# A sum of two weight quarters made by an accumulating GpSimd DMA instead of a VectorE add

## The chip, the core and the metric

One core of one Trainium2 chip runs the whole program. The metric is the device time of one launch in microseconds (us); lower is better. TensorE multiplies, VectorE (DVE), ScalarE (ACT) and GpSimd (POOL) work on data in SBUF and PSUM, and DMA queues bring data from HBM; SyncE (SP) issues nearly all of the loads.

## What is computed

Two layers of a streaming encoder over 528 tokens (16 meta tokens and 512 real ones) with 1024 channels. Each layer is a gated feed-forward network (FFN), a mixer and a second FFN. So there are four FFNs, and they hold most of the work:

```python
def swiglu(h, w_gate, w_up, w_down):
    return (jax.nn.silu(h @ w_gate) * (h @ w_up)) @ w_down
...
    for layer in range(DEPTH):
        g = norm_gains[layer]
        h = h + 0.5 * swiglu(rmsnorm(h, g[0]), ffn_w_gate[layer, 0], ffn_w_up[layer, 0], ffn_w_down[layer, 0])
        u = rmsnorm(h, g[1])
...
        h = h + mix
        h = h + 0.5 * swiglu(rmsnorm(h, g[2]), ffn_w_gate[layer, 1], ffn_w_up[layer, 1], ffn_w_down[layer, 1])
    return rmsnorm(h, final_norm)[:, N_META:]
```

`D_FF` is 2816, in 22 blocks of 128 columns. All data is float32.

## The kernel before

**Groups.** The gate and up products of an FFN go in two passes, `groups(q, p)` for FFN `q` = 0 to 3 and half `p` = 0 or 1; behind each pass stands `down(q, p)`, the part of the down projection that it feeds. A pass works on groups of two blocks of `D_FF`. A pass with `p` = 0 has five groups, one with `p` = 1 has six; the very first pass has two. The first group of a pass is the one that `leads(g)` names. In a group, each weight matrix (gate, and up beside it) is cut into four quarters `a11`, `a21`, `a22`, `a12` of 128 by 1024 in SBUF, and seven products take the place of eight: `p1` takes `a11`, `p2` takes `a12`, `p4` takes `a22`, and four take sums of quarters: `p7` takes `s3 = a11 + a21` (line 1252 or 1255), `p5` takes `s1 = a21 + a22` (line 1270), `p6` takes `s2 = a11 + s1` (line 1276) and `p3` takes `s4 = a12 + s2` (line 1303). Each product is made once for the gate (`n = 2g`) and once for up (`n = 2g + 1`), so a group holds 14.

**Splits.** A weight that TensorE reads is held as a high part, which ScalarE copies into a shorter float type (`wh`; functions `high_...`), and a low part, the difference, which VectorE makes (`wl`; functions `low_...`). A product is 12 matmuls: four pieces of the contraction, three parts each. So each of the six forms costs a ScalarE copy and a VectorE difference, and the four sums cost a VectorE add each.

**Buffers.** The quarters arrive in a ring of four slots, `raw`. In every group but the first of a pass, `s3` goes to the scratch row `ws[:, 5]`, `s1` is then added in place onto `a21` in `raw`, `s2` in place onto `a11`, and `s4` into another row of `ws`. SyncE loads a quarter of the next group into a slot as soon as its old content is done with: `a11` behind `s4`, `a21` behind `low_s1`, `a22` behind `low_a22`, `a12` behind `p2`.

**Order.** There is no scheduler: each engine's list is written by hand, and semaphores that count tie them. In an inner group `g` VectorE goes through `low_s2(g)`, `low_s1(g)`, `sum_s4(g)`, the split of `a12`, work on PSUM results and on the hidden rows, `low_s4(g)`, `low_a22(g)`, `low_a11(g+1)`, `sum_s3(g+1)`, `gate_a_out(g)` (1456), `sum_s1(g+1)`, `sum_s2(g+1)`, `low_s3(g+1)`, `c21` (1452), `gate_b_scale` (1466), and in the next round `c22` (1445). TensorE's order in an inner group is `p1(n)`, `p7(n)`, `p3(n-1)`, `p6(n)`, `p4(n-1)`, `p2(n)`, `p5(n)`, `p1(n+1)`, `p7(n+1)`, `p3(n)`, `p6(n+1)`, `p4(n)`, `p2(n+1)`, `p5(n+1)`. ScalarE goes, from the middle of the group: `high_s3` (623), three PSUM copies, the silu of the gate (804), `high_s2(g+1)` (630), the second silu (810), `high_s1(g+1)` (638), `p1_copy` (721), the split of `a12` (661).

**What `p6(n)` waits for.** `s2_low` (the low part of `s2`) and `p1_copied` (ScalarE's copy at line 721, which stands behind `high_s1` in its list). GpSimd's list in the FFNs holds only `clear_ss`, a memset of the row of squares, which waits for the norm before it.

Of the kernel before, what the change touches and what calls it, by code (L numbers as in the profile page):

```python
# [6 lines left out]
ALU = mybir.AluOpType  # L7
# [18 lines left out]
CHUNKS_UP = 2 * FT  # L26
# [59 lines left out]
def leads(g):  # L86

    return g == GROUP[PASS_OF[g]][0]
# [22 lines left out]
def leading(g):  # L111

    return sum(leads(h) for h in range(g + 1))


def ring_place(kind, g):
# [88 lines left out]
def trunk(nc, x_dram, gains, w_gu, w_dn, ev_in, ev_out, od_in, od_out, conv_w, sinks, rel_bias, gate_b, pool_w,  # L205
          pool_scale, ident_in, onehot_in, causal_in, sel_in, out):
    table_dram = nc.dram_tensor("bias_table", [P, 8, TABLE], F32, kind="Internal").ap()
    with ExitStack() as ctx:
# [3 lines left out]
        def sem(name):  # L212
            return ctx.enter_context(nc.semaphore(name))
# [174 lines left out]
        form_ready, first_ready, u_added = sem("form_ready"), sem("first_ready"), sem("u_added")  # L388
        down_front, down_back, down_scaled = sem("down_front"), sem("down_back"), sem("down_scaled")
        table_kept = sem("table_kept")  # L390
        a12_split, b21_split = sem("a12_split"), sem("b21_split")

        block = ctx.enter_context(nc.Block())
# [181 lines left out]
        def _(act):  # L575
# [54 lines left out]
                act.activation(wh[:, form_slot("s2", g), :], raw_quarter("a11", g), ACT.Copy).then_inc(s2_high, 1)  # L630

            def high_s1(g):
                act.wait_ge(s1_sum, g + 1)
                if leads(g):
                    act.activation(wh[:, 5, :], ws[:, 5, :], ACT.Copy).then_inc(s1_high, 1)
                else:
                    act.wait_ge(p7_done if leads(g - 1) else p5_done, 2 * g)
                    act.activation(wh[:, form_slot("s1", g), :], raw_quarter("a21", g), ACT.Copy).then_inc(s1_high, 1)

# [488 lines left out]
        def _(pool):  # L1128
# [8 lines left out]
            def clear_ss(v):  # L1137
                if v:
                    pool.wait_ge(stat_done, v)
                pool.memset(ss[:, :], 0.0).then_inc(ss_zero, 1)  # L1140
                pool.wait_ge(ss_zero, v + 1)

            clear_ss(0)
            clear_ss(1)

            pool.memset(zbuf[:, 0:2], 0.0).then_inc(pool_step, 1)
            steps[0] += 1
            pool.wait_ge(pool_step, steps[0])
            for s in range(EV_TILES):
# [14 lines left out]
                if s >= 7 and (s - 7) % 3 == 0:  # L1164
                    j = (s - 7) // 3
                    pool.wait_ge(acc_free, TILE["ev_in"] + s + 1)
                    pool.tensor_tensor(zbuf[:, 2:2 + L], conv_c[:, :], conv_x[:, :], ALU.mult).then_inc(z_ready, 1)
            clear_ss(2)
            clear_ss(3)
            clear_ss(4)  # L1170

            for s in range(OD_TILES):
# [27 lines left out]
                                       ALU.subtract).then_inc(pool_ready, 1)  # L1200
            pool.wait_ge(yd_l, 4)
            clear_ss(5)
            clear_ss(6)
            pool.wait_ge(x_gained, KT - 1)
            for h, (a, b) in enumerate(ENDS):
# [6 lines left out]
        def _(dve):  # L1212
# [34 lines left out]
            def sum_s3(g):  # L1247
                dve.wait_ge(raw_in[raw_slot("a11", g)], RAW_COUNT["a11", g])
                dve.wait_ge(raw_in[raw_slot("a21", g)], RAW_COUNT["a21", g])
                if leads(g):  # L1250
                    dve.wait_ge(s1_sum, g + 1)
                    dve.tensor_tensor(raw_quarter("a21", g), raw_quarter("a11", g), raw_quarter("a21", g), ALU.add).then_inc(s3_sum, 1)
                else:
                    dve.wait_ge(p5_done if leads(g - 1) else p7_done, 2 * g)
                    dve.tensor_tensor(ws[:, 5, :], raw_quarter("a11", g), raw_quarter("a21", g), ALU.add).then_inc(s3_sum, 1)
# [7 lines left out]
            def sum_s1(g):  # L1263
                dve.wait_ge(raw_in[raw_slot("a21", g)], RAW_COUNT["a21", g])
                dve.wait_ge(raw_in[raw_slot("a22", g)], RAW_COUNT["a22", g])
                if not leads(g):
                    dve.wait_ge(s3_sum, g + 1)
                elif g:
                    dve.wait_ge(p7_done, 2 * g)
                dve.tensor_tensor(s1_full(g), raw_quarter("a21", g), raw_quarter("a22", g), ALU.add).then_inc(s1_sum, 1)  # L1270

            def sum_s2(g):
                dve.wait_ge(s1_sum, g + 1)
                dve.wait_ge(s3_sum, g + 1)
                dve.wait_ge(a11_low, g + 1)
                dve.tensor_tensor(raw_quarter("a11", g), raw_quarter("a11", g), s1_full(g), ALU.add).then_inc(s2_sum, 1)
# [209 lines left out]
            def groups(q, p):  # L1486
# [4 lines left out]
                for g in range(first, end):  # L1491
                    if g == first:
                        low_a22(g)
                        low_a11(g + 1)
                        sum_s3(g + 1)
                        if q and not p:
                            norm(V_FFN[q], real)
                        sum_s1(g + 1)
                        if p:
                            sum_s2(g + 1)  # L1500
                        c22(2 * g, real)
                        c22(2 * g + 1, real)
                        if not p:
                            sum_s2(g + 1)
                        c21(2 * g, real)
                        low_s3(g + 1)
                        gate_a_out(g, real)
                        low_s2(g + 1)
                        c21(2 * g + 1, real)
                        gate_b_scale(g, real)  # L1510
                        continue
# [21 lines left out]
                        sum_s3(g + 1)  # L1533
                    gate_a_out(g, real)
                    if g + 1 < end:
                        sum_s1(g + 1)
                        sum_s2(g + 1)
                        low_s3(g + 1)
                    else:
                        low(n)  # L1540
                    c21(2 * g, real)
                    gate_b_scale(g, real)
                    if q and not p and g == first + 1:
                        low_b21(q, real)
# [1083 lines left out]
```

## Time and profile before

| | before |
|---|---|
| median of 3 runs | 1822.62 us (1822.48 to 1823.01) |
| the profiled execution, first to last instruction (span) | 1821.0 us |
| busy: TensorE, VectorE, ScalarE, GpSimd | 1801.7, 1344.8, 859.6, 53.1 us |
| granted TensorE clock, mean | 0.998 of full |
| `in_w_gate_up` quarter loads issued by SyncE | 175 of 512 KB |

No device time of the profiled execution is given apart from its span; the median of the runs lies 1.6 us above that span. A timeline row gives the start, the duration, the engine, the line and the tiles; brackets hold the idle time of that engine just before it and what ended it. Starts of neighbouring VectorE rows are less than a duration apart, because the next instruction starts while the last one ends.

### The profile page before, as it was taken

The page shows a single profiled execution, that of the slowest core. Times are in us where ns is not written, and L with a number is a line of the kernel's source. Part 1 is how long each engine was busy: PE and PEld are TensorE (multiplying, and loading weights), DVE is VectorE, ACT ScalarE, POOL GpSimd, SP SyncE. Part 2 cuts the span into 40 slices and gives each one's busy share as a digit, 9 for nine tenths or more (in the row PEclk, how much of TensorE's full clock was granted, in tenths as well). Part 3 has the DMA queues.
Part 4 walks back from the last instruction along what each step waited for, and adds up shares of the span by engine and source line. Part 5 has one row for each costly group of instructions (what it writes and reads, how often), then busy time and mean ns, then how long its engine had stood idle before and what let it go on. Part 6 is the DMA issues. An engine that isn't in the chain of part 4 may idle for free.

```text
span 1821.0 us, 32718 instructions
## 1 busy us (share of the span) xinstructions
PE 1801.7 (99%) x13456; PEld 1720.7 (94%) x13456; DVE 1344.8 (74%) x1814; ACT 859.6 (47%) x1404; POOL 53.1 (3%) x68
## 2 busy tenths in 40 slices
PE   8999999999999999999999999999999999999997
PEld 8999999999999999999999999999998899889986
DVE  7766887557778966896798578855656799568954
ACT  8443464335446543554555335534423565335542
POOL 0000000000000000000000000000124000000000
PEclk9999999999999999999999999999999999999999
DMA  5255233341222333233223322333312223332331
GB/s 179 85 96 116 95 115 108 102 135 59 70 70 82 101 99 108 89 105 105 82 93 108 97 98 97 107 112 112 93 59 70 70 82 105 102 106 93 111 111 57
DMA packets 81107, 176.87 MB, mean 97 GB/s; under 512 B 7292, under 2 KB 12700, under 8 KB 80960
## 3 DMA queue, kind: packets, MB, share of 16 engines
q1 hardware_dynamic: 80544, 174.49, 31.3%
q8 instruction: 108, 1.77, 0.4%
q14 instruction: 39, 0.32, 0.1%
q10 hardware_dynamic: 416, 0.29, 0.0%
HBM read 171.35 MB, written 3.41 MB: 96 GB/s over the span
## 4 chain that ended last, share of the span: by engine, by line
PE 96%; DVE 2%; ACT 1%; DMA 0%; SPq 0%; issue 0%; DVEq 0%; ACTq 0%
PE psum L2028 25%; PE psum L2098 13%; PE psum L2100 13%; PE psum L2101 13%; PE psum L2038 7%; PE psum L2037 4%; PE psum L2041 4%; PE psum L2036 4%; PE psum L2040 3%; PE psum L2148 2%; PE psum L2147 2%; PE psum L2149 2%; PE psum L2157 2%; DMA rb_sb<-in_rel_bias 0%; DVE rms L1391 0%; PE psum L2336 0%
## 5 line engine op out<-in xcount | busy, mean ns | idle before, releaser
L2098 PE MATMUL psum<-fh,wh 128*128 128x264 f32 (+1 forms) x1968 | 559.9, 285 | 2.2 <-ACT psum L728 2.2
L2101 PE MATMUL psum<-fh,wl 128*128 128x264 f32 (+1 forms) x1968 | 557.2, 283 | 0.0
L2100 PE MATMUL psum<-fl,wh 128*128 128x264 f32 (+1 forms) x1968 | 556.7, 283 | 0.0
L2098 PEld LDWEIGHTS psum<-fh,wh 128*128 128x128 f32 x1968 | 371.1, 189 | 3.5 <-issue 3.0
L2100 PEld LDWEIGHTS psum<-fl,wh 128*128 128x128 f32 x1968 | 370.9, 188 | 0.6
L2101 PEld LDWEIGHTS psum<-fh,wl 128*128 128x128 f32 x1968 | 369.8, 188 | 0.0
L588 ACT ACTIVATE wh<-raw 128x1024 fp32r<-128x1024 f32 (+2 forms) x194 | 169.2, 879 | 224.1 <-PE psum L2028 172.7
L2028 PE MATMUL psum<-xs,wh 128*128 128x264 f32 (+1 forms) x1504 | 267.3, 297 | 5.0 <-DVE xs L1341 3.5
L1226 DVE TENSOR_TENSOR wl<-raw,wh 128x1024 fp32r<-128x1024 f32 (+2 forms) x193 | 194.7, 1016 | 95.8 <-ACT wh L588 95.1
L2028 PEld LDWEIGHTS psum<-xs,wh 128*128 128x128 f32 x1504 | 213.7, 189 | 15.6 <-issue 5.2
L2038 PE MATMUL psum<-hs,wh 128*128 128x512 f32 x528 | 206.6, 391 | 0.0
L2028 PE MATMUL psum<-hs,wh 128*128 128x512 f32 (+2 forms) x760 | 192.3, 349 | 0.0
L2028 PE MATMUL psum<-xs,wl 128*128 128x264 f32 (+1 forms) x736 | 161.9, 294 | 0.0
L2037 PE MATMUL psum<-hs,wh 128*128 128x272 f32 x528 | 152.5, 289 | 0.0
L2041 PE MATMUL psum<-hs,wl 128*128 128x272 f32 x528 | 151.3, 287 | 0.0
L2036 PE MATMUL psum<-hs,wh 128*128 128x272 f32 x528 | 150.6, 285 | 0.0
L2040 PE MATMUL psum<-hs,wl 128*128 128x256 f32 x528 | 147.6, 280 | 0.0
L2028 PEld LDWEIGHTS psum<-hs,wh 128*128 128x128 f32 x760 | 128.4, 188 | 20.0
L2028 PE MATMUL psum<-hs,wl 128*128 128x512 f32 (+2 forms) x380 | 122.9, 351 | 0.0
L2041 PEld LDWEIGHTS psum<-hs,wl 128*128 128x128 f32 x528 | 99.1, 188 | 22.1
L2028 PEld LDWEIGHTS psum<-xs,wl 128*128 128x128 f32 x736 | 116.6, 188 | 2.7
L2038 PEld LDWEIGHTS psum<-hs,wh 128*128 128x128 f32 x528 | 100.2, 190 | 0.0
(314 smaller groups left out, 3000.4 us busy)
## 6 DMA issues: line engine op xcount, KB each, us to landing
raw<-in_w_gate_up SPq DMA_DIRECT2D x175, 512.0 KB, 3.7
raw<-in_w_down SPq DMA_DIRECT2D x64, 384.0 KB, 3.2
raw<-in_w_down SPq DMA_DIRECT2D x64, 320.0 KB, 3.0
raw<-in_od_in SPq DMA_DIRECT2D x21, 512.0 KB, 3.5
raw<-in_ev_in SPq DMA_DIRECT2D x18, 512.0 KB, 3.5
raw<-in_ev_out SPq DMA_DIRECT2D x8, 512.0 KB, 3.5
raw<-in_od_out SPq DMA_DIRECT2D x8, 512.0 KB, 3.5
x<-in_x_t SPq DMA_DIRECT2D x8, 264.0 KB, 4.9
```

Of the source, the lines that this page charges most:

```text
L588: act.activation(wh[:, slot, 0:w], raw[:, slot, 0:w], ACT.Copy).then_inc(wh_ready, 1)
L1226: dve.tensor_tensor(wl[:, slot, 0:w], raw[:, slot, 0:w], f32(wh[:, slot, 0:w]), ALU.subtract).then_inc(wl_ready, 1)
L2028: last = pe.matmul(dst, weights[:, slot, w], both[:, at, part, tok], start=start and p == 0, stop=stop and p == len(steps) - 1)
L2036: pe.matmul(a, wh[:, slot, w], both[:, k, 0, 0:FRONT], start=start, stop=False)
L2037: pe.matmul(a, wh[:, slot, w], both[:, k, 1, 0:FRONT], start=False, stop=False)
L2038: pe.matmul(psum[:, 2 * acc_at + 1, :].rearrange("p (h t) -> p h t", h=2), wh[:, slot, w], both[:, k, :, b], start=start, stop=False, skip ...
L2040: pe.matmul(back(acc_at, 0), wl[:, slot, w], both[:, k, 0, b], start=False, stop=stop, skip_group_check=True)
L2041: return pe.matmul(a, wl[:, slot, w], both[:, k, 0, 0:FRONT], start=False, stop=stop)
L2098: pe.matmul(psum[:, bank, 0:w], wh[:, slot, cols], high_x, start=start and j == 0, stop=False, skip_group_check=True)
L2100: pe.matmul(psum[:, bank, 0:w], wh[:, slot, cols], low_x, start=False, stop=False, skip_group_check=True)
L2101: last = pe.matmul(psum[:, bank, 0:w], wl[:, slot, cols], high_x, start=False, stop=j == 3, skip_group_check=True)
L2147: pe.matmul(psum[:, 4 * s, 0:w], a12_in(g)[:, cols], high_x, start=False, stop=False, skip_group_check=True)
```

## The change

In every group but the first of a pass (33 of 41 groups), the add `s1 = a21 + a22` is taken out of VectorE's list. In its place GpSimd waits until `s3` of that group has been made (since `s3` reads the plain `a21`) and issues a DMA that reads the `a22` quarter from HBM once more and adds it onto `a21` in SBUF. Those that read `s1` (`sum_s2` on VectorE and `high_s1` on ScalarE) wait for the semaphore of this DMA, `s1_added`. The plain `a22` is still loaded, for `p4`. `sum_s2` moves back in VectorE's list: behind `c21` in an inner group, behind both `c22` in the first group of a pass. The semaphore `s1_sum` now counts leading groups only.

```diff
+def following(g):
+    return g + 1 - leading(g)
...
             def high_s1(g):
-                act.wait_ge(s1_sum, g + 1)
                 if leads(g):
+                    act.wait_ge(s1_sum, leading(g))
                     act.activation(wh[:, 5, :], ws[:, 5, :], ACT.Copy).then_inc(s1_high, 1)
                 else:
+                    act.wait_ge(s1_added, 16 * following(g))
...
+            def accumulate(q, p):
+
+                first, count = GROUP[q, p]
+                for g in range(first + 1, first + count):
+                    at = q * CHUNKS_UP + 2 * (group_f(g) + 1)
+                    pool.wait_ge(s3_sum, g + 1)
+                    pool.dma_start(raw[:, raw_slot("a21", g), :].rearrange("p (s c) -> p s c", s=2),
+                                   w_gu[at:at + 2, :, 512:1024].rearrange("s p c -> p s c"),
+                                   accum_op=ALU.add).then_inc(s1_added, 16)
...
             def sum_s2(g):
-                dve.wait_ge(s1_sum, g + 1)
+                if leads(g):
+                    dve.wait_ge(s1_sum, leading(g))
+                else:
+                    dve.wait_ge(s1_added, 16 * following(g))
...
                         sum_s3(g + 1)
                         if q and not p:
                             norm(V_FFN[q], real)
-                        sum_s1(g + 1)
-                        if p:
-                            sum_s2(g + 1)
                         c22(2 * g, real)
                         c22(2 * g + 1, real)
-                        if not p:
-                            sum_s2(g + 1)
+                        sum_s2(g + 1)
                         c21(2 * g, real)
...
                     gate_a_out(g, real)
                     if g + 1 < end:
-                        sum_s1(g + 1)
-                        sum_s2(g + 1)
                         low_s3(g + 1)
                     else:
                         low(n)
                     c21(2 * g, real)
+                    if g + 1 < end:
+                        sum_s2(g + 1)
                     gate_b_scale(g, real)
```

The lines of the changed kernel are numbered otherwise: 1255 is 1280 (`s3`), 1276 is 1302 (`s2`), 1281 is 1307 (`low_s3`), 1286 is 1312 (`low_s2`), 1292 is 1318 (`low_s1`), 1445 is 1471, 1452 is 1478, 1456 is 1482, 1466 is 1492.

VectorE's list in an inner group of a pass, from the sum `s3` to `low_s1`. Before:

```order
L1255 TENSOR_TENSOR ws<-raw 128x1024
L1456 TENSOR_TENSOR gate<-psum,rms 128x528
L1270 TENSOR_TENSOR raw<-raw 128x1024
L1276 TENSOR_TENSOR raw<-raw 128x1024
L1281 TENSOR_TENSOR wl<-ws,wh 128x1024
L1452 TENSOR_TENSOR spare<-spare,psum 128x264
L1466 TENSOR_TENSOR spare<-spare,rms 128x528
L1445 TENSOR_TENSOR spare<-spare,psum 128x264
L1286 TENSOR_TENSOR wl<-raw,wh 128x1024
L1292 TENSOR_TENSOR wl<-raw,wh 128x1024
```

and in the changed kernel:

```order
L1280 TENSOR_TENSOR ws<-raw 128x1024
L1482 TENSOR_TENSOR gate<-psum,rms 128x528
L1307 TENSOR_TENSOR wl<-ws,wh 128x1024
L1478 TENSOR_TENSOR spare<-spare,psum 128x264
L1302 TENSOR_TENSOR raw<-raw 128x1024
L1492 TENSOR_TENSOR spare<-spare,rms 128x528
L1471 TENSOR_TENSOR spare<-spare,psum 128x264
L1312 TENSOR_TENSOR wl<-raw,wh 128x1024
L1318 TENSOR_TENSOR wl<-raw,wh 128x1024
```

The two rows of the old list that write `raw<-raw` are `s1` and `s2`; one is gone, and `s2` now stands two rows further back, in front of `gate_b_scale`.

VectorE's list in the first group of a pass with `p` = 1, from `s3` on. Before:

```order
L1255 TENSOR_TENSOR ws<-raw 128x1024
L1270 TENSOR_TENSOR raw<-raw 128x1024
L1276 TENSOR_TENSOR raw<-raw 128x1024
L1441 TENSOR_TENSOR psum<-psum,spare 128x264
L1445 TENSOR_TENSOR spare<-spare,psum 128x264
L1441 TENSOR_TENSOR psum<-psum,spare 128x264
L1445 TENSOR_TENSOR spare<-spare,psum 128x264
L1452 TENSOR_TENSOR spare<-spare,psum 128x264
L1281 TENSOR_TENSOR wl<-ws,wh 128x1024
```

and in the changed kernel:

```order
L1280 TENSOR_TENSOR ws<-raw 128x1024
L1467 TENSOR_TENSOR psum<-psum,spare 128x264
L1471 TENSOR_TENSOR spare<-spare,psum 128x264
L1467 TENSOR_TENSOR psum<-psum,spare 128x264
L1471 TENSOR_TENSOR spare<-spare,psum 128x264
L1302 TENSOR_TENSOR raw<-raw 128x1024
L1478 TENSOR_TENSOR spare<-spare,psum 128x264
L1307 TENSOR_TENSOR wl<-ws,wh 128x1024
```

Here `s2` moves from in front of the two pairs of `c22` rows to behind them.

GpSimd's list around the second and third FFN, from the first mixer to the start of the second. Before:

```order
L1167 ISA
L1167 TENSOR_TENSOR spare<-conv_c,conv_x 128x528 x4
L1140 MEMSET ss 128x528 x3
L1175 MEMSET v_tok 128x5
L1176 MEMSET row_parts 36x1536
```

and in the changed kernel:

```order
L1186 TENSOR_TENSOR spare<-conv_c,conv_x 128x528 x4
L1147 MEMSET ss 128x528
L1156 DMA raw<-in_w_gate_up 128x2x512 x9
L1147 MEMSET ss 128x528
L1156 DMA raw<-in_w_gate_up 128x2x512 x9
L1147 MEMSET ss 128x528
L1198 MEMSET v_tok 128x5
L1199 MEMSET row_parts 36x1536
```

Nine accumulating DMAs now stand between the memsets, each of which had followed the last one directly.

## Rows read from the trace of the kernel before

**Rows 1.** The page, part 1: busy time, share, instructions of each engine.

```profile
PE 1801.7 (99%) x13456; PEld 1720.7 (94%) x13456; DVE 1344.8 (74%) x1814; ACT 859.6 (47%) x1404; POOL 53.1 (3%) x68
```

**Rows 2.** The page, part 4: the chain that ended last, by engine.

```profile
PE 96%; DVE 2%; ACT 1%; DMA 0%; SPq 0%; issue 0%; DVEq 0%; ACTq 0%
```

**Rows 3.** Waits of TensorE, the one entry inside the FFNs: us, times, longest.

```profile
PE psum L2098 <- ACT psum L728: 2.2, 4, 0.6
```

**Rows 4.** Timeline of TensorE: the second of the four waits for line 728.

```profile
742.52 0.36 PE L2098 MATMUL psum<-fh,wh 128*128 128x264 f32 x1 [0.56 <-ACT psum L728]
```

**Rows 5.** Timeline of VectorE, one inner group and the next: start, us.

```profile
609.68 1.22 DVE L1255 TENSOR_TENSOR ws<-raw 128x1024 f32<-128x1024 f32 x1
...
612.18 1.23 DVE L1270 TENSOR_TENSOR raw<-raw 128x1024 f32<-128x1024 f32 x1 [0.66 <-DMA raw<-in_w_gate_up]
613.44 1.23 DVE L1276 TENSOR_TENSOR raw<-raw 128x1024 f32<-128x1024 f32 x1
614.58 1.22 DVE L1281 TENSOR_TENSOR wl<-ws,wh 128x1024 fp32r<-128x1024 f32 x1
...
618.54 1.23 DVE L1292 TENSOR_TENSOR wl<-raw,wh 128x1024 fp32r<-128x1024 f32 x1 [0.19 <-ACT wh L638]
620.27 1.23 DVE L1303 TENSOR_TENSOR ws<-raw 128x1024 f32<-128x1024 f32 x1 [0.51 <-PE psum L2101]
...
630.10 1.22 DVE L1255 TENSOR_TENSOR ws<-raw 128x1024 f32<-128x1024 f32 x1
```

**Rows 6.** Timeline of ScalarE in the same group.

```profile
614.76 1.06 ACT L630 ACTIVATE wh<-raw 128x1024 fp32r<-128x1024 f32 x1 [1.36 <-DVE raw L1276]
616.92 0.65 ACT L810 ACTIVATE spare<-spare 128x528 f32<-128x528 f32 x1 [1.10 <-DVE spare L1466]
617.47 1.04 ACT L638 ACTIVATE wh<-raw 128x1024 fp32r<-128x1024 f32 x1
618.42 0.37 ACT L721 ACTIVATE psum<-psum 128x264 f32<-128x264 f32 x1
```

**Rows 7.** Timeline of TensorE: first matmul of a product `p2`.

```profile
623.00 0.28 PE L2147 MATMUL psum<-fl,high 128*128 128x264 f32 x1
```

**Rows 8.** Timeline of SyncE's queue: the load of `a22` for the next group.

```profile
608.60 0.37 SPq L485 DMA_DIRECT2D raw<-in_w_gate_up  x1
```

**Rows 9.** Windows, while that load moves: us, busy by engine, PEclk, DMA share, GB/s.

```profile
609.50:612.00 2.50, 2.50 (x23) 2.50 (x22) 2.02 (x3) 1.06 (x2) 0.00 (x0) 1.00 0.65 213
```

**Rows 10.** Page part 6 and DMA view: KB each, median us from issue to landing.

```profile
raw<-in_w_gate_up SPq DMA_DIRECT2D x175, 512.0 KB, 3.7
...
bias_table<-sq SPq DMA_DIRECT2D x8, 160.0 KB, 8.6
```

**Rows 11.** Timeline of GpSimd: a product of two 528-element rows.

```profile
451.37 1.31 POOL L1167 TENSOR_TENSOR spare<-conv_c,conv_x 128x528 f32<-128x528 f32 x1 [25.52 <-DVE conv_x L1396]
```

**Rows 12.** Groups by line, VectorE: the sum `s1` where it is added in place.

```profile
L1270 DVE TENSOR_TENSOR raw<-raw 128x1024 f32<-128x1024 f32 x33 | 40.4, 1225 | 18.4 <-DMA raw<-in_w_gate_up 17.8
```

**Rows 13.** Timeline of VectorE: end of `s3`, then `s4`, in a pass of five groups.

```profile
588.97 1.22 DVE L1255 TENSOR_TENSOR ws<-raw 128x1024 f32<-128x1024 f32 x1
...
599.86 1.22 DVE L1303 TENSOR_TENSOR ws<-raw 128x1024 f32<-128x1024 f32 x1 [0.67 <-PE psum L2101]
```

**Rows 14.** The same in a pass of six groups, `s3` of its second group first.

```profile
726.49 1.22 DVE L1255 TENSOR_TENSOR ws<-raw 128x1024 f32<-128x1024 f32 x1
...
748.31 1.22 DVE L1255 TENSOR_TENSOR ws<-raw 128x1024 f32<-128x1024 f32 x1
...
760.29 1.23 DVE L1303 TENSOR_TENSOR ws<-raw 128x1024 f32<-128x1024 f32 x1 [1.58 <-PE psum L2101]
```

**Rows 15.** Timeline of VectorE, last FFN: `s3`, `s4`, next `s3`.

```profile
1517.55 1.22 DVE L1255 TENSOR_TENSOR ws<-raw 128x1024 f32<-128x1024 f32 x1
...
1527.83 1.23 DVE L1303 TENSOR_TENSOR ws<-raw 128x1024 f32<-128x1024 f32 x1
...
1537.50 1.22 DVE L1255 TENSOR_TENSOR ws<-raw 128x1024 f32<-128x1024 f32 x1
```

More of the change, by code:

```diff
@@ L390, in trunk @@
         table_kept = sem("table_kept")
+        s1_added = sem("s1_added")
         a12_split, b21_split = sem("a12_split"), sem("b21_split")
@@ L1141, in clear_ss @@
                 pool.wait_ge(ss_zero, v + 1)
+            def accumulate(q, p):
[6 more added lines that the diff above has]
+                                   accum_op=ALU.add).then_inc(s1_added, 16)
             clear_ss(0)
             clear_ss(1)
+            accumulate(0, 0)
+            accumulate(0, 1)
             pool.memset(zbuf[:, 0:2], 0.0).then_inc(pool_step, 1)
@@ L1168, in _ @@
             clear_ss(2)
+            accumulate(1, 0)
+            accumulate(1, 1)
             clear_ss(3)
+            accumulate(2, 0)
+            accumulate(2, 1)
             clear_ss(4)
@@ L1202, in _ @@
             clear_ss(5)
+            accumulate(3, 0)
+            accumulate(3, 1)
             clear_ss(6)
@@ L1265, in sum_s1 @@
                 dve.wait_ge(raw_in[raw_slot("a22", g)], RAW_COUNT["a22", g])
-                if not leads(g):
-                    dve.wait_ge(s3_sum, g + 1)
-                elif g:
+                if g:
                     dve.wait_ge(p7_done, 2 * g)
@@ L1272, in sum_s2 @@
             def sum_s2(g):
-                dve.wait_ge(s1_sum, g + 1)
+                if leads(g):
+                    dve.wait_ge(s1_sum, leading(g))
+                else:
+                    dve.wait_ge(s1_added, 16 * following(g))
                 dve.wait_ge(s3_sum, g + 1)
```

## The prediction

> **What bounds the kernel now.** I read the page's busy times first: TensorE is busy 1801.7 of 1821.0 us, VectorE 74% of the span [rows 1]. The chain that ended last gives TensorE 96% and VectorE 2% [rows 2]. In the list of what TensorE waited for, one entry lies inside the FFNs: 2.2 us in four places, for ScalarE's copy at line 728, which the change doesn't touch [rows 3]. So this kernel can hardly win by lighter work on VectorE. It can lose, if something that TensorE reads comes late. The question is one of slack, and the timeline of an inner group answers it.
>
> **The slack in an inner group.** I take as zero the end of `s3`, since that is what the accumulating DMA waits for: 609.68 + 1.22 = 610.90 [rows 5]. The next `s3` starts 20.42 us behind this one (630.10 - 609.68) [rows 5]; with 14 products that is 1.46 us for one. `p2(n)` starts at 623.00 [rows 7] and two products (`p6`, `p4`) stand between, so `p6(n)` starts at 620.08, which is +9.2. VectorE reaches `s4` at 620.27, after 0.51 us of waiting for TensorE [rows 5].
>
> Call S the time from zero until `sum_s2` can start. Today it starts at 613.44, +2.5, with the plain `s1` ahead of it. Two paths leave from it.
>
> To `p6`: from the start of `s2` to that of `high_s2` 614.76 - 613.44 = 1.32; then, start to start, 0.95 for that copy (as 618.42 - 617.47), 0.55 for the second silu (617.47 - 616.92), 0.95 for `high_s1`, and 0.37 for `p1_copy` [rows 5, 6]. That is S + 4.14, some S + 4.2 with the signal. `p6` needs it at +9.2, so it is late where S is over 5.0.
>
> Back to the next `s3`: `low_s1` waits for `high_s1`, whose end is S + 1.32 + 0.95 + 0.55 + 1.04 = S + 3.9, and holds VectorE 1.14 us (as 614.58 - 613.44) [rows 5, 6]. So `s4` can start at S + 5.04. From the start of `s4` to the end of the next `s3` VectorE takes 630.10 + 1.22 - 620.27 = 11.05 us [rows 5], which I take as work without slack. The round is then S + 16.1 against TensorE's 20.42: over S = 4.3 each group makes the next one later, and it adds up.
>
> **What is removed.** 33 adds of 1.225 us, 40.4 us of VectorE, and 17.8 us of its waits for the plain `a22` [rows 12]. They lie beside matmuls, and TensorE isn't waiting for them: worth nothing. The earlier `low_s3` (behind `gate_a_out` now, instead of at 614.58 [rows 5]) serves `p7`, which doesn't wait either.
>
> **What is added: S.** No row shows an accumulating DMA, or any DMA from GpSimd. The nearest is SyncE's load of the same quarter: issued at 608.60 [rows 8], and VectorE took the data at 612.18 [rows 5]: 3.6 us. While it moved, the 16 engines were 0.65 busy for 2.5 us, or 1.6 us of all of them [rows 9]. Low end: the add costs nothing beside a plain load, S = 3.6. A second read, of the old `a21` out of SBUF, can hide or cost another 1.6 us: S up to 5.2. On top comes the making of the descriptors in GpSimd's software, between nothing and the 1.3 us that GpSimd takes for an ordinary instruction [rows 11]; I take the middle, 0.7. High end: the slowest transfer in the trace, made of many small pieces, 8.6 us [rows 10]. The new one has the shape of the plain load, so it is nearer to the low end. I take the second read in full, 3.6 + 1.6 + 0.7: S = 5.9.
>
> The Trainium skill ("Collectives: The Full Stack", The bandwidth ceiling) says that a DMA add is slowed by its two source reads and not by the adding, and runs at half the rate of a copy; that speaks for the 1.6 us, and no run here shows it yet. The Trainium skill ("DMA: Bandwidth & Descriptors", Anatomy of one DMA, SWDGE path) fits 2.0 us plus the bytes at 436 GB/s; as an estimate from that page, with the bytes counted twice, S would be 4.4 and the kernel would stay where it is, against my 31 us of loss. This is the rival below that is called covered.
>
> **The sum.** A pass of five groups has four accumulating DMAs. The first of them belongs to the second group, whose `s2` stands behind the norm or the `c22` rows, with more room: in a pass of six TensorE waits up to 742.52 for the copy in front of `p5(n)` [rows 4], so `p6(n)`, one product and 0.56 earlier, starts at 740.5, and `s3` of that group ended at 727.7 [rows 14]: 12.8 us, where S + 4.5 is used (`s2`, `c21`, `low_s3`, `gate_a_out`, `low_s2`). I take no loss there, in both kinds of pass. The next may use 599.86 - 590.19 - 5.04 = 4.6 us [rows 13]; the third 4.3; the last has no next `s3` behind it and only `p6` to serve, 5.0. Loss: 3S - 13.9. In a pass of six the second may use 760.29 - 749.53 - 5.04 = 5.7 [rows 14], and one more inner group follows: 4S - 19.3 where S is over 5.7, else 3S - 13.6. In the last FFN the round is 19.95 (1537.50 - 1517.55) and VectorE's part 10.89 [rows 15], so each of its seven terms is 0.3 larger: 2.3 in all. There are three passes of five and four of six.
> At S = 5.9: 3 x 3.8 + 4 x 4.3 + 2.3 = 31 us. At 5.2: 3 x 1.7 + 4 x 2.0 + 2.3 = 15. At 3.6: nothing. At 8.6: 3 x 11.9 + 4 x 15.1 + 2.3 = 98. The profiled span would be 1821.0 + 31 = 1852; the median of the runs stands 1.6 above the profiled span, so 1853.5.
>
> **Moves that I cost at nothing.** Behind the waiting `s2` VectorE has `gate_b_scale`, `c22`, `low_s2` and `low_s1`. `c22` is due for `p3(n-1)` one product ahead of `p6`, at +7.7, and done by about S + 2.6: late only over S = 5.1, in the shadow of `p6`, which is then later still. ScalarE has its second silu, `high_s1` and `p1_copy` behind `high_s2`: counted. On GpSimd's list a memset of `ss` may now wait behind nine DMAs, but is first needed in the down stage behind them. The load of `a12` is issued when `p2(n+1)` of the group before ends, seven products ahead of 623.00 and one long: +3.4. Even with 1.6 us of sharing it lands at +8.6, and its copy (1.0) and difference (1.2) end at +10.9, ahead of `p2(n)` at +12.1. The extra 33 x 512 KB of reads fall where the DMA engines are otherwise idle.
>
> **Rivals.**
> Covered (16%): S stays under 4.7, because the second read overlaps the first and descriptors are cheap. For it: a plain load takes 3.6 [rows 5, 8]. Against it: either of the two extra costs alone, at the size I take for the read, uses the room of 1.1 us. Time: 1822.6, up to 3 us more. It lies on the other side of my forecast; the point that decides is S = 4.7.
> Far slower (20%): S over 7.5, descriptors or the adding cost several us. By the sum 71 us and up: from 1893 on. For it: the 8.6 us row [rows 10]; against it: those were small pieces.
> Faster (2%): the four waits for line 728 [rows 3] vanish, 2.2 us: 1820. ScalarE's list there doesn't change.
> Slower as worked out (62%): S from 4.7 to 7.5, 1826 to 1893.
>
> **How the numbers follow.** A difference under 0.2% (3.6 us) is about what a measurement can't tell from none here. Same is the covered case, 0.16; slower is 0.62 + 0.20 = 0.82; faster 0.02. The range takes in the covered case and the likeliest and leaves out the far slower one but its nearest part: 1822 to 1895, with some 0.2 outside. The likeliest case's own range is 1826 to 1893.
>
> **What the changed profile would show.** S: from the end of the row at line 1280 to the start of that at 1302 in inner groups, 5.9, with some 3 us of idle time before 1302 put down to a DMA, where the old sum had 0.66 [rows 5]. The loop: inner `s3` rows 22.0 apart in place of 20.4. TensorE: new waits, 1 to 1.6 us in each inner group, for ScalarE's copy at `p1_copy` or VectorE's `low_s2`, and none in first groups. VectorE: busy 40 us less. I am wrong if S is under 4.7; if the rounds stay at 20.4 with S well above it (then the 11.05 has slack that I took for work); or if TensorE waits elsewhere, for `p7` or `p3`.

## The result, and the profile after

The changed kernel takes 1881.14 us (median of 4 runs, 1880.01 to 1883.97); the kernel before took 1822.82 us on the same chip (1822.48 to 1823.19). The ratio is 1.0321, with an interval of 1.0307 to 1.0336: the change costs 58 us. The forecast was 1853.5 with a range of 1822 to 1895, so the sign and the range hold, and the loss is nearly twice the 31 us that the sum gave.

The page of the changed kernel, busy times and the chain that ended last (compare [rows 1, 2]):

```profile
PE 1824.3 (97%) x13456; PEld 1728.3 (92%) x13456; DVE 1304.0 (69%) x1781; ACT 857.4 (46%) x1404; POOL 93.0 (5%) x101
...
PE 64%; DVE 15%; DMA 10%; issue 6%; ACT 4%; SPq 0%; DVEq 0%; ACTq 0%; POOLq 0%
```

VectorE is 40.8 us lighter, as worked out, and the kernel is slower by more than that. The chain that was 96% TensorE now runs through VectorE, a DMA and issue. The granted clock was 0.997 (0.998 before); 0.001 of the 1821 us is 1.8 us, an estimate, so the clock is not the cause.

What TensorE waited for, after: us in all, times, longest (before, only the entry of [rows 3] lay inside the FFNs):

```profile
PE psum L2120 <- DVE spare L1471: 21.1, 22, 2.1
PE psum L2120 <- DVE gate L1482: 6.5, 4, 4.4
PE psum L2120 <- ACT psum L728: 4.9, 19, 0.3
...
PE psum L2169 <- DVE raw_low L1343: 1.1, 6, 0.2
```

`c22` (1471) stands behind `sum_s2` in VectorE's list, `p1_copy` (728) behind `high_s2`: the waits are those of things queued behind the sum that waits. `gate_a_out` (1482) is behind `s2` only in the first groups of passes. These rows hold 34 us. The span grew by 57.9: TensorE's idle time by 35.3 and its busy time by 22.6 (1824.3 against 1801.7). The ends of matmuls are modelled in this profile, so the waits show the places of the loss, and the distances of the `s3` rows show its size.

VectorE in one inner group of the third FFN, after (start, us; the same rows of before are [rows 5]):

```profile
1181.10 1.22 DVE L1280 TENSOR_TENSOR ws<-raw 128x1024 f32<-128x1024 f32 x1
...
1184.59 0.42 DVE L1478 TENSOR_TENSOR spare<-spare,psum 128x264 f32<-128x264 f32 x1
1188.41 1.23 DVE L1302 TENSOR_TENSOR raw<-raw 128x1024 f32<-128x1024 f32 x1 [3.40 <-DMA raw<-in_w_gate_up]
1189.55 0.70 DVE L1492 TENSOR_TENSOR spare<-spare,rms 128x528 f32<-128x528 f32 x1
...
1192.30 1.22 DVE L1318 TENSOR_TENSOR wl<-raw,wh 128x1024 fp32r<-128x1024 f32 x1 [0.26 <-ACT wh L645]
1193.45 1.22 DVE L1329 TENSOR_TENSOR ws<-raw 128x1024 f32<-128x1024 f32 x1
...
1203.22 1.22 DVE L1280 TENSOR_TENSOR ws<-raw 128x1024 f32<-128x1024 f32 x1
```

GpSimd in the same group, and the windows around it (us, busy by engine, PEclk, DMA share, GB/s):

```profile
1182.62 1.21 POOL L1156 DMA_DIRECT2D raw<-in_w_gate_up  x1 [21.01 <-DVE ws L1280]
```

```profile
1182.50:1184.50 2.00, 2.00 (x19) 2.00 (x18) 1.49 (x2) 2.00 (x5) 1.21 (x1) 1.00 0.26 97
1184.50:1188.50 4.00, 4.00 (x35) 4.00 (x35) 0.60 (x3) 0.30 (x1) 0.00 (x0) 1.00 1.00 197
```

`s3` ends at 1182.32 and `s2` starts at 1188.41: S = 6.09. Of it, 0.3 us pass until GpSimd starts, GpSimd is busy for 1.21, and then the 16 DMA engines are busy throughout for 4 us. Not all of that is the add: at 197 GB/s the 4 us hold 0.79 MB, and SyncE's load of `a12`, issued at 1185.92, takes part of them. Over the program one add takes 3.3 us of all 16 engines (5.8% of 1878.9 us, by 33). VectorE idles 3.40 us for the DMA. `s4` starts S + 5.04 after zero (1193.45), and the next `s3` starts 22.12 us behind this one, which is S + 16.03; before it was 20.42, with TensorE setting the pace. Over the 33 accumulating DMAs the median of S is 6.20; in the 25 that are not the first of their pass it averages 6.33; in the first of the program it is 12.70.

The page's DMA parts, after: queue, packets, MB, share of 16 engines; and the landing in us (before: [rows 10]):

```profile
q0 software_dynamic: 8976, 17.30, 5.8%
...
raw<-in_w_gate_up POOLq DMA_DIRECT2D x33, 512.0 KB, 5.8
```

### The profile page after: what moved, and what is told of

Its sections match the earlier page's. It is cut to its first block, busy times and chain, and to the rows that moved or that the text cites. A ratio compares the mean times of both kernels' runs of the same rounds, so it can differ in the third digit from the quotient of the medians.

```text
span 1878.9 us, 32686 instructions
## 1 busy us (share of the span) xinstructions
PE 1824.3 (97%) x13456; PEld 1728.3 (92%) x13456; DVE 1304.0 (69%) x1781; ACT 857.4 (46%) x1404; POOL 93.0 (5%) x101
## 3 DMA queue, kind: packets, MB, share of 16 engines
q0 software_dynamic: 8976, 17.30, 5.8%
## 4 chain that ended last, share of the span: by engine, by line
PE 64%; DVE 15%; DMA 10%; issue 6%; ACT 4%; SPq 0%; DVEq 0%; ACTq 0%; POOLq 0%
PE psum L2050 24%; DMA raw<-in_w_gate_up 10%; PE psum L2060 6%; PE psum L2120 4%; PE psum L2122 4%; PE psum L2123 4%; PE psum L2059 4%; PE psum L2063 3%; PE psum L2058 3%; PE psum L2062 3%; DVE ws L1280 2%; DVE raw_low L1343 2%; DVE raw L1302 1%; DVE wl L1339 1%; PE psum L2179 1%
## 5 line engine op out<-in xcount | busy, mean ns | idle before, releaser
L2120 PE MATMUL psum<-fh,wh 128*128 128x264 f32 (+1 forms) x1968 | 566.5, 288 | 35.0 <-DVE spare L1471 21.1
L2050 PEld LDWEIGHTS psum<-hs,wh 128*128 128x128 f32 x760 | 128.4, 188 | 20.1
L636 ACT ACTIVATE wh<-raw 128x1024 fp32r<-128x1024 f32 x41 | 43.4, 1058 | 168.1 <-DVE raw L1302 168.1
```

The lines of the kernel that those rows point to most:

```text
L2050: last = pe.matmul(dst, weights[:, slot, w], both[:, at, part, tok], start=start and p == 0, stop=stop and p == len(steps) - 1)
L2120: pe.matmul(psum[:, bank, 0:w], wh[:, slot, cols], high_x, start=start and j == 0, stop=False, skip_group_check=True)
```

## The experiments

S (from the end of `s3` to the start of `s2`) and the round (from one `s3` to the next) are read as above, in each kernel's own trace: S as the median of 33, the round as the median of the 13 inner ones of the first three FFNs. The ratios of e1 to e10 are to the kernel before as it ran beside each of them, 1823.25 to 1823.51 us. The theory throughout: S is long because the add needs a second read, and the round is the larger of TensorE's 20.42 and S + 16.1. The rivals: GpSimd as issuer is the cost; the moved `s2` is the cost; a first-use cost; and all of the loss lies in the inner rounds.

| kernel | median us | ratio to before, interval | S, median | round, median | first S |
|---|---|---|---|---|---|
| before | 1822.82 | 1 | 2.60 | 20.42 | 7.22 |
| changed | 1881.14 | 1.0321 (1.0307 to 1.0336) | 6.20 | 22.24 | 12.70 |
| e1 no add, GpSimd | 1827.78 | 1.0024 (1.0015 to 1.0034) | 4.27 | 20.42 | 9.65 |
| e2 no add, SyncE | 1824.59 | 1.0007 (0.9998 to 1.0017) | 4.16 | 20.42 | 7.22 |
| e3 `s2` moved only | 1823.59 | 1.0001 (0.9992 to 1.0011) | 4.04 | 20.42 | 7.23 |
| e4 `s3` ahead of both lows | 1902.77 | 1.0435 (1.0419 to 1.0450) | 7.86 | 22.99 | 12.22 |
| e5 earlier first use | 1882.12 | 1.0325 (1.0307 to 1.0342) | 6.25 | 22.29 | 12.68 |
| e6 table store later | 1876.73 | 1.0293 (1.0277 to 1.0308) | 6.33 | 22.39 | 7.75 |
| e7 half the bytes | 1828.24 | 1.0029 (1.0017 to 1.0040) | 4.39 | 20.51 | 10.04 |
| e8 two pieces of cover | 1857.28 | 1.0188 (1.0173 to 1.0203) | 6.29 | 21.47 | 12.91 |
| e9 e8, e6, first groups | 1848.19 | 1.0139 (1.0122 to 1.0156) | 6.38 | 21.44 | 8.98 |
| e10 e9, gate row ahead | 1853.20 | 1.0164 (1.0147 to 1.0181) | 6.21 | 21.28 | 9.59 |

**e1, the DMA without its add.** The same DMA from the same queue at the same place, as a copy: `s1` then holds `a22` alone, and the kernel computes something else.

```diff
-                                   w_gu[at:at + 2, :, 512:1024].rearrange("s p c -> p s c"),
-                                   accum_op=ALU.add).then_inc(s1_added, 16)
+                                   w_gu[at:at + 2, :, 512:1024].rearrange("s p c -> p s c")).then_inc(s1_added, 16)
```

> The GpSimd DMA copies a22 over a21 and adds nothing, so that s1 holds a22 alone; all else is as in the changed kernel. Theory (the second read is what makes the accumulating DMA long, and the loss is a loop of length S + 16.1 against TensorE's 20.4): without the read of the old a21 the engines move for 1.6 us less, S falls from 6.2 to about 4.5, inner rounds from 22.2 to 20.6, and the time to 1825 to 1832. Rival (GpSimd's software is what is slow, the add is free): S stays near 6, rounds at 22, time over 1870.

The queue's row and the landing of e1, from the page; then GpSimd and VectorE in an inner group:

```profile
q0 software_dynamic: 4752, 17.30, 3.1%
...
raw<-in_w_gate_up POOLq DMA_DIRECT2D x33, 512.0 KB, 3.9
```

```profile
612.95 0.72 POOL L1156 DMA_DIRECT2D raw<-in_w_gate_up  x1 [20.07 <-DVE ws L1279]
```

```profile
611.43 1.22 DVE L1279 TENSOR_TENSOR ws<-raw 128x1024 f32<-128x1024 f32 x1
616.90 1.23 DVE L1301 TENSOR_TENSOR raw<-raw 128x1024 f32<-128x1024 f32 x1 [1.55 <-DMA raw<-in_w_gate_up]
...
631.85 1.22 DVE L1279 TENSOR_TENSOR ws<-raw 128x1024 f32<-128x1024 f32 x1
```

Without the add S is 4.25 here (616.90 - 612.65) and the round is back at 20.42. For the same 17.30 MB the queue used 3.1% of the DMA engines' time in place of 5.8%, 57 us in place of 109, and 4752 packets in place of 8976. So the add costs 1.9 us of S: 0.5 in GpSimd's row (0.72 against 1.21) and the rest while the data moves. In engine time it is 1.6 us for each of the 33. The run shows the price of the add; that a second read makes it is a reading, borne out by the packets. The Trainium skill ("Collectives: The Full Stack", The bandwidth ceiling) says of ReduceScatter that its add needs two source reads and so runs at half the rate of a copy; the trace agrees, with 1.9 times the engines' time (109 / 57). What is left of the loss (4.5 us; 3.9 between the profiled spans) lies where S is still too long: 1.8 in the first pass, 2.1 in the last FFN, whose round of 19.95 is shorter than S + 15.9 (its rounds there are 20.17).

**e2, the same copy from SyncE.** GpSimd issues nothing; the copy stands behind SyncE's load of `a22`.

```diff
+                        if kind == "a22" and not leads(g):
+                            sp.wait_ge(s3_sum, g + 1)
+                            sp.dma_start(raw[:, raw_slot("a21", g), :].rearrange("p (s c) -> p s c", s=2),
+                                         w_gu[at:at + 2, :, half:half + 512].rearrange("s p c -> p s c")).then_inc(s1_added, 16)
...
-                    pool.wait_ge(s3_sum, g + 1)
-                    pool.dma_start(raw[:, raw_slot("a21", g), :].rearrange("p (s c) -> p s c", s=2),
```

> The same copy of a22 over a21 (again no add), issued by SyncE behind its wait for s3 and ahead of the load of a12; GpSimd issues nothing. Theory: S is 3.6 to 4.0, below the 4.3 of the loop, and the time is that of before, 1822 to 1825. Rival (the extra 17 MB of reads or the moved s2 cost time by themselves): 1830 or more with S under 4.3.

1824.59 against 1827.78: where only a copy is made, going by GpSimd costs 3.2 us. Some 1.8 of them lie in the first pass, where SyncE's copy goes ahead of the table's store in its own list, so that S is 7.22 and not 9.65. The 3.2 us isn't GpSimd's share of the 58: with S under 4.3 a longer S costs nothing. In the 25 groups that aren't first in their pass S averages 3.92 here and 4.34 in e1; above the threshold those 0.4 us would count in each, some 10 us, an estimate. The rival that GpSimd's software is the main cost falls all the same, since with GpSimd issuing a copy e1 loses 4.5 us. What the 0.5 us by which its row is longer for an add cost alone is not shown; they are a part of the add's 1.9.

**e3, only the order.** The kernel before, with `s1` still on VectorE and `sum_s2` where the change puts it.

```diff
                         sum_s1(g + 1)
-                        sum_s2(g + 1)
                         low_s3(g + 1)
                     else:
                         low(n)
                     c21(2 * g, real)
+                    if g + 1 < end:
+                        sum_s2(g + 1)
```

> The kernel before, with VectorE's s1 kept where it was and only s2 moved as in the change, behind c21 and behind both c22. Theory: s2 starts about 1.5 us later than before in inner groups (+3.9), below the 4.3 of the loop, so 1822 to 1825. Rival (the moved s2 takes a part of the 58 us): 1828 or more.

A ratio of 1.0001. `s2` starts about 4.0 us after the end of `s3` in place of 2.5, and the round stays at 20.41. The move alone costs nothing, as it should with S under 4.3.

**e4, `s3` earlier.** If the loop is VectorE's, `s3` ahead of `low_a22` and `low_a11` should take two differences out of it.

```diff
                     c22(2 * g, real)
+                    if g + 1 < end:
+                        sum_s3(g + 1)
                     low_a22(g)
                     if g + 1 < end:
                         low_a11(g + 1)
-                        sum_s3(g + 1)
                     gate_a_out(g, real)
```

> The changed kernel, with s3 of the next group made ahead of low_a22 and low_a11 on VectorE in inner groups, so that these two lie in the shadow of the DMA. Theory: the loop is shorter by two instructions of 1.14 us, S + 13.8 = 20.0 at S = 6.2, just under TensorE's 20.4; what stays is the first group of the program (6 us) and those of the passes with six groups (some 5 us): 1832 to 1842. Rival (each group is late by itself, or the DMA slows other transfers): VectorE's order changes little, over 1865.

A plain miss: 1902.77 where 1832 to 1842 was expected. VectorE in e4, an inner group, and the landings:

```profile
628.22 1.23 DVE L1280 TENSOR_TENSOR ws<-raw 128x1024 f32<-128x1024 f32 x1 [1.23 <-PE psum L2124]
...
637.37 1.23 DVE L1302 TENSOR_TENSOR raw<-raw 128x1024 f32<-128x1024 f32 x1 [3.56 <-DMA raw<-in_w_gate_up]
...
651.21 1.23 DVE L1280 TENSOR_TENSOR ws<-raw 128x1024 f32<-128x1024 f32 x1 [1.23 <-PE psum L2124]
```

```profile
raw<-in_w_gate_up SPq DMA_DIRECT2D x175, 512.0 KB, 4.4
...
raw<-in_w_gate_up POOLq DMA_DIRECT2D x33, 512.0 KB, 7.5
```

Two things had been left out. `low_a22` releases SyncE's next load of 512 KB; behind `s3` it starts with the accumulation, and both are slower (7.5 us to landing in place of 5.8, 4.4 in place of 3.8), so S is 7.92 here. And `s3` may not start ahead of TensorE's second `p7` of the group before, whose start hangs on `s2` too: the next `s3` ends at 651.21 + 1.23, which is 23.0 behind the end of this one, S + 15.1. So there is a second loop, through TensorE, at S + 15.0 to 15.1, and cover can take only about 1 us off a round.

**e8, `s3` ahead of `low_a11` and the second `hidden_low`.** It leaves `low_a22`, and with it SyncE's load, in front.

```diff
                     low_s4(g)
-                    hidden_low(g - 1, real, 1)
                     c22(2 * g, real)
                     low_a22(g)
                     if g + 1 < end:
+                        sum_s3(g + 1)
                         low_a11(g + 1)
-                        sum_s3(g + 1)
+                    hidden_low(g - 1, real, 1)
```

> The changed kernel, with s3 of the next group ahead of low_a11 and of the second hidden_low on VectorE, but behind low_a22, so that SyncE's load of a22 starts as early as it did (in the run with both lows moved it started behind s3, shared the engines with the accumulation, and S rose to 7.9). Sharing as the cause of that rise: S is 6.1 to 6.6, VectorE's loop is S + 14.4 and TensorE's own way from p6 to the next s3 gives S + 15.0, as there: rounds of 21.2, and some 25 x 1.0 us less than the changed kernel, 1853 to 1862. If S rises again to 7 or more, or the rounds stay at 22, the reading of that run is wrong: 1875 and more.

VectorE in e8: `s3`, `s2`, and the next `s3`.

```profile
619.87 1.23 DVE L1280 TENSOR_TENSOR ws<-raw 128x1024 f32<-128x1024 f32 x1 [0.55 <-PE psum L2123]
...
627.42 1.23 DVE L1302 TENSOR_TENSOR raw<-raw 128x1024 f32<-128x1024 f32 x1 [2.48 <-DMA raw<-in_w_gate_up]
...
641.27 1.23 DVE L1280 TENSOR_TENSOR ws<-raw 128x1024 f32<-128x1024 f32 x1 [0.55 <-PE psum L2123]
```

S is 6.32 (627.42 - 621.10), the round 21.40, which is S + 15.1; `s3` waits for TensorE in it, as in e4, but the loads are out of the way. Of the 58 us 24 come back, and 1857.28 is within the expectation.

**e5, an earlier first use.** A small accumulating DMA of 8 KB at the program's start, to see whether the first one's 12.70 us is a first-use cost.

```diff
+            link(pool.memset(pool_pad[:, :], 0.0))
+            pool.dma_start(pool_pad[:, :], ident_in[:, 0:16], accum_op=ALU.add).then_inc(s1_added, 16)
```

> The changed kernel with one tiny accumulating GpSimd DMA (8 KB onto a spare tile) at the start of the program, long before the first real one, whose S was 12.7 where the others have 6.0 to 7.8. If the first one is slow because the queue or its software is used for the first time, S of the first falls to 6 or 7 and the time by some 6 us, to 1875. If it is slow because it shares the DMA engines with SyncE's stores of the bias table, S stays at 12 to 13 and the time at 1881.

It isn't: S in the first pass is still 12.68 us. The rival is what moves beside it. SyncE's queue at that place, in the changed kernel, and VectorE there:

```profile
91.79 0.37 SPq L491 DMA_DIRECT2D raw<-in_w_gate_up  x1
92.21 0.58 SPq L499 DMA_DIRECT2D bias_table<-sq  x1
```

```profile
90.37 1.22 DVE L1280 TENSOR_TENSOR ws<-raw 128x1024 f32<-128x1024 f32 x1
...
104.29 1.22 DVE L1302 TENSOR_TENSOR raw<-raw 128x1024 f32<-128x1024 f32 x1 [5.39 <-DMA raw<-in_w_gate_up]
```

**e6, the table's store later.** The first store of `bias_table` waits for the first accumulation.

```diff
                         sp.wait_ge(table_kept, 1)
+                        if i == 0:
+                            sp.wait_ge(s1_added, 16)
```

> The changed kernel, with SyncE's first store of the bias table (many small pieces) held back until the first accumulating DMA has landed. Sharing as the cause: S of the first falls from 12.7 to 6 or 7.5, the time by some 5 us, to 1876. First use as the cause: S stays over 11, 1881.

VectorE in e6: `s3` ends at 91.12, and `s2` hardly waits for the DMA.

```profile
89.90 1.22 DVE L1282 TENSOR_TENSOR ws<-raw 128x1024 f32<-128x1024 f32 x1
...
98.87 1.22 DVE L1304 TENSOR_TENSOR raw<-raw 128x1024 f32<-128x1024 f32 x1 [0.45 <-DMA raw<-in_w_gate_up]
```

S is 7.75 in place of 12.70, and the kernel is 4.4 us faster than the changed one. In the kernel before S is 7.22 at this place, since the two `c22` pairs stand ahead of `s2` there. In the trace of e6 the first pass loses nothing any more (the `s3` of the second pass starts at 190.9, against 191.1 before and 197.4 in the changed kernel); the gain of the whole is smaller because S of some later first groups is longer in this run, 8.59 and 8.02 in place of 7.75 and 6.51. Why is open.

**e7, half the bytes.** The accumulation takes the gate's half of the quarter alone; the up half of `s1` is left as `a21`, so this kernel too computes something else.

```diff
-                    pool.dma_start(raw[:, raw_slot("a21", g), :].rearrange("p (s c) -> p s c", s=2),
-                                   w_gu[at:at + 2, :, 512:1024].rearrange("s p c -> p s c"),
+                    pool.dma_start(raw[:, raw_slot("a21", g), 0:512],
+                                   w_gu[at, :, 512:1024],
```

> The accumulating DMA adds only the gate half of a22 (256 KB); the up half of s1 lacks its a22. If the bytes, counted twice, make the length, S falls by half of 3.3 us, from 6.2 to 4.5, inner rounds are 20.6 and the time 1824 to 1830. If a fixed cost of the adding path makes it, S stays over 5.5 and the time over 1860.

S falls from 6.20 to 4.39 and the round to 20.51: just over 4.3, and just at the edge where the forecast puts it. So 256 KB added are worth 1.8 us of S, and by the same line zero bytes would leave about 2.6 us, an estimate.

**e9, three places together.** e8 and e6, and in the first groups of passes `s2` two rows further back:

```diff
                         c22(2 * g, real)
                         c22(2 * g + 1, real)
-                        sum_s2(g + 1)
                         c21(2 * g, real)
                         low_s3(g + 1)
+                        sum_s2(g + 1)
                         gate_a_out(g, real)
```

The expectation calls this last edit "the gate row ahead of s2", in passes with `p` = 1. The kernel that ran is that of the diff: `s2` stands behind `c21` and `low_s3`, still ahead of the gate row, in all eight passes.

> Three edits on the changed kernel at once: s3 ahead of the second pair of hidden-row sums and of low_a11 (as in the run with two pieces of cover), the first store of the bias table behind the first accumulation, and in the first groups of the passes with p = 1 the gate row (line 1482) ahead of s2, so that it no longer waits for the accumulation. Theory: three places lose time apart from the loop. The run with two pieces of cover stands at 1857.3, 34 us over the kernel before. The table store was worth 4.4 us; the first groups of four passes some 5.3 us together. So 1857.3 - 4.4 - 5.3 = 1847.5, between 1844 and 1852; inner rounds still 21.2 to 21.5, since those come from TensorE's product p7(n+1), which s3 follows. In first groups TensorE's waits for line 1482 (7.1 us in 6 places in that run) fall under 2 us. Rival: the first groups' loss is not the gate row's but that of s2 itself for p6; then they keep it and the time is 1852 to 1854, with the waits of TensorE put down to another line. Further rival: the three edits move the start of other loads and take back what they give, 1857 or more.

1848.19, as expected, 9.1 us under e8. Read pass by pass against e8, 5.9 of it come in the first pass and some 3 in the other seven. TensorE's waits for the gate row, 7.1 us in 6 places in e8, are gone from its list; what leads it in e9:

```profile
PE psum L2122 <- ACT psum L730: 3.5, 13, 0.4
PE psum L2052 <- DVE xs L1369: 3.4, 5, 1.1
PE psum L2122 <- DVE spare L1473: 3.3, 6, 0.9
```

Still, in all eight passes the way from the pass's first `s4` to its second takes 0.64 us or more longer than in the kernel before. So the first groups' loss isn't the gate row's alone.

**e10, the gate row really ahead of `s2`.** On top of e9:

```diff
                         low_s3(g + 1)
-                        sum_s2(g + 1)
                         gate_a_out(g, real)
+                        sum_s2(g + 1)
```

> The run before (all covers) was announced with the gate row ahead of s2 in the first groups of the passes with p = 1; what it in fact did was to put s2 behind c21 and low_s3, still ahead of the gate row. Here the gate row really stands ahead of s2, and nothing else differs from it. Theory: the waits of TensorE for the gate row are already gone there, since c21 and low_s3 (1.5 us) now run while the DMA moves; the gate row ended at 8.9 us after zero where it had ended at 9.9, in the first such group. Then s2 is what is late next, and the gate row ahead of it costs s2 0.6 us where the DMA has already landed and nothing where it hasn't. Time 1847 to 1850, no difference from 1848.2. Rival: the first groups still lose 0.65 to 1 us each because p1 of the second group reads behind the gate row without a wait being shown; then 1845 or less.

1853.20 (ratio 1.0164, 1.0147 to 1.0181): 5 us slower than e9, outside the expectation. The same place of the second pass, VectorE in e9 and then in e10:

```profile
191.07 1.22 DVE L1282 TENSOR_TENSOR ws<-raw 128x1024 f32<-128x1024 f32 x1
...
199.29 1.22 DVE L1304 TENSOR_TENSOR raw<-raw 128x1024 f32<-128x1024 f32 x1
200.43 0.70 DVE L1484 TENSOR_TENSOR gate<-psum,rms 128x528 f32<-128x528 f32 x1
```

```profile
192.10 1.22 DVE L1282 TENSOR_TENSOR ws<-raw 128x1024 f32<-128x1024 f32 x1
...
200.38 0.70 DVE L1484 TENSOR_TENSOR gate<-psum,rms 128x528 f32<-128x528 f32 x1
200.99 1.22 DVE L1304 TENSOR_TENSOR raw<-raw 128x1024 f32<-128x1024 f32 x1
```

S is 7.67 in e10 and 7.00 in e9. The price of 0.6 us was in the expectation; that each of the eight first groups pays it (8 x 0.6 = 4.8) was not, since I took `s2` to have room there once the gate row was served. It has none: on the way from the first `s4` of a pass to its second each of the eight loses 0.3 to 0.6 us against e9 (seven of them 0.6). TensorE's waits for line 730 (`p1_copy`) grow from 3.5 us in 13 places to 8.0 in 19.

No version beats the kernel before. There TensorE already sets the pace, so the most that a DMA in place of `s1` can reach is that pace.

## Why the prediction came out as it did

**What bounds, and the slack.** Right. e1, e2, e3 and e7 have a median S from 4.0 to 4.4 and a round of 20.4 to 20.5; the changed kernel has 6.20 and 22.24, with a longest inner S of 7.63 and a round of 23.69 behind it. The forecast's S + 16.1 is measured as S + 16.03, and its threshold of 4.3 lies where e7 begins to show 20.5 (at S = 4.46 and 4.48). That 40 us less of VectorE gain nothing is shown too: e1 has them, and gains nothing. One reading of its own sum is off: at S = 4.7, which it calls the end of the covered case with up to 3 us of loss, its terms add up to about 6.

**S.** Near, and a little small: 5.9 forecast, 6.20 the median, 6.33 the mean of the 25 accumulations that aren't first in their pass. Two of the three terms hold nearly to the tenth: load and descriptors were 3.6 + 0.7 = 4.3, and the copy of e1 has S = 4.27; the second read was 1.6, and the DMA engines are busy 1.6 us longer for each add. What the forecast lacked is that GpSimd's own row is 0.5 us longer for an add than for a copy (1.21 against 0.72); in all, the add costs 1.9 us of S (e1). Put into the forecast's own sum, S = 6.33 gives 3 x 5.1 + 4 x 6.0 + 2.3 = 42, which is 11 of the 27 us that were missing. The "covered" rival needed S under 4.7, and the add alone rules it out. So the estimate of 4.4 that was drawn from the Trainium skill ("DMA: Bandwidth & Descriptors", Anatomy of one DMA, SWDGE path) was too short by 1.8 us here, even with the bytes counted twice.

**"I take no loss there", in first groups.** This step failed, in two places. In the first pass 6.0 us were lost: the accumulation ran beside the small pieces of the table's store, and S was 12.70 us; e6 took the loss of that pass away, e5 ruled out a first use. In the four passes of six groups the first groups lost 0.7 to 2.0 us each, 5.2 in all, read at the next `s4`; one pass of five groups lost 0.6 there. The forecast had followed `s2` to `p6`, and not along VectorE's own list to `s4`, as it did for inner groups. In a pass of six, `s2` and then `s4` behind it, after, and that `s4` before:

```profile
747.25 1.22 DVE L1280 TENSOR_TENSOR ws<-raw 128x1024 f32<-128x1024 f32 x1
...
755.59 1.23 DVE L1302 TENSOR_TENSOR raw<-raw 128x1024 f32<-128x1024 f32 x1 [1.52 <-DMA raw<-in_w_gate_up]
...
762.66 1.21 DVE L1329 TENSOR_TENSOR ws<-raw 128x1024 f32<-128x1024 f32 x1
```

```profile
740.44 1.22 DVE L1303 TENSOR_TENSOR ws<-raw 128x1024 f32<-128x1024 f32 x1
```

S is 7.12 (755.59 - 748.47) and `s4` starts at 14.19, S + 7.07; before it stood at 12.73 (740.44 - 727.71). All four passes have S + 7.0 to 7.1 after, and 12.5 to 12.8 before, so such a group is late from S = 5.4 to 5.7 on, and already at the 5.9 that was forecast. A second row that the forecast didn't follow is the gate row behind `s2`, whose PSUM bank `p1(n)` of the second group needs. TensorE waits for it in the first pass and in three of the four passes of six; the fourth loses 0.7 us without such a wait, and e9, where these waits are gone, still loses 0.64 us or more in each:

```profile
107.75 0.56 PE L2120 MATMUL psum<-fh,wh 128*128 128x264 f32 x1 [4.40 <-DVE gate L1482]
...
208.66 0.36 PE L2120 MATMUL psum<-fh,wh 128*128 128x264 f32 x1 [0.36 <-DVE gate L1482]
...
759.05 0.37 PE L2120 MATMUL psum<-fh,wh 128*128 128x264 f32 x1 [0.53 <-DVE gate L1482]
...
1689.65 0.35 PE L2120 MATMUL psum<-fh,wh 128*128 128x256 f32 x1 [1.20 <-DVE gate L1482]
```

**"The last has ... only `p6` to serve, 5.0".** Mis-sized. Measured, the last link of a pass costs about S - 4.33 like the others, 0.67 more, seven times: 4.7 us. The last one of the sixth pass, where S is 6.49, shows why. TensorE, and VectorE's difference of `a12`:

```profile
1213.26 0.36 PE L2120 MATMUL psum<-fh,wh 128*128 128x264 f32 x1 [0.94 <-DVE spare L1471]
...
1215.21 0.36 PE L2120 MATMUL psum<-fh,wh 128*128 128x264 f32 x1 [0.24 <-ACT psum L728]
...
1218.09 0.28 PE L2123 MATMUL psum<-fh,wl 128*128 128x264 f32 x1
1218.47 0.36 PE L2169 MATMUL psum<-fl,high 128*128 128x264 f32 x1
```

```profile
1217.10 1.22 DVE L1343 TENSOR_TENSOR raw_low<-raw,high 128x1024 fp32r<-128x1024 f32 x1
```

`p6` starts 10.77 after the end of `s3` (1215.21 - 1204.44) where before it was 9.2: 1.57 late, the S - 5.0 + 0.1 of the forecast. But `p2(n)` then waits too, until 1218.32, when `raw_low` is done: that is S + 7.4, because the split of `a12` stands behind `low_s1` and `s4` in VectorE's list. The forecast took its end from the kernel before (+10.9). Matmuls start 0.12 us apart; here 1218.47 follows 0.38 behind 1218.09, and behind each restart the next matmul comes 0.20 later. This is read from rows; no run tests it apart.

**The account.** 31 forecast, 11 for S, 6 in the first pass, 5.2 in first groups, 4.7 in last links: 57.9. The profiled spans differ by 1878.9 - 1821.0 = 57.9. Such a fit to a tenth is partly luck: the terms overlap by some tenths each, and the 0.6 us of the one pass of five is in none of them.

**TensorE's waits.** Their sum in an inner group is 0.7 to 2.3 us where 1 to 1.6 was forecast, and first groups, which were to have none, have four; the place of most is one product earlier, at `p3(n-1)` for `c22`, where the forecast had said that this would lie in the shadow of `p6`. Since `c22` comes first, it takes the greater part of the wait, and `p6` the rest.

## What to carry to other kernels

Before moving an add into a DMA, look not at whether the vector engine is busy but at how soon the sum is needed behind the last read of its old content: here 4.3 us were to be had, a copy took 4.3 and an add 6.2, and the inner groups each paid the difference. Follow every row that is queued behind the waiting one to its reader, and the waiting engine's own list back to the next row that starts the DMA, in the first and the last group of a loop as well, since a loop that repeats pays one threshold and its ends pay others. And when a wait is covered by moving work, ask which loads that work releases: in e4 this cost more than the cover gave.

## What the runs showed of the hardware

- An accumulating DMA of 512 KB from HBM onto SBUF took 5.8 us from issue to landing, the same as a copy 3.9; it used 1.9 times the DMA engines' time and 8976 packets against 4752. GpSimd's row was 1.20 us against 0.72 (medians).
- With half the bytes (256 KB) the add took 4.1 us to landing; the 8 KB one of e5, at the program's start, 5.2 us.
- Transfers of two queues slow each other. With a 512 KB load of SyncE's beside it the add took 7.5 us in place of 5.8 and the loads 4.4 in place of 3.8 (e4); beside the table's store S was 12.70 in place of 7.75 (e6). The Trainium skill ("DMA: Bandwidth & Descriptors", Issuing engines are not separate DMA queues) says that DMAs of all issuing engines run on the same 16 engines and interleave; the trace agrees, with those numbers.
